# Second block's up projections: one 512-column matmul for the high and the low activations

## The reference

```python
for l in range(DEPTH_2):                      # DEPTH_2 = 2
    ...
    h = rmsnorm_2(x, norm_mlp[l])
    u = jax.nn.relu(jnp.einsum('bsd,df->bsf', h, w_up[l]))      # 2048 -> 8192
    x = x + jnp.einsum('bsf,fd->bsd', u * u, w_down[l])         # 8192 -> 2048
```

## Time and profile before

| | |
|---|---|
| Median of three runs | 3373.12 us (3364.39 to 3373.55) |
| Profiled execution, span from first to last instruction | 3372.1 us |
| TensorE busy (matmuls) | 3234.7 us, 96% |
| VectorE busy | 2239.3 us, 66% |
| ScalarE busy | 1423.9 us, 42% |
| Matmuls | 27278 |
| Mean granted clock of TensorE | 0.973 of full speed |

### The profile page before, as it was taken

The page is one execution under the profiler, slowest core; times in us unless marked ns, Lnnn a source line. Parts: engine busy times, 40 slices in busy tenths (PEclk is TensorE's granted clock), DMA queues, the critical chain, the costliest instruction groups (busy, mean ns, idle before and its releaser), DMA issues.

```text
span 3372.1 us, 63513 instructions
## 1 busy us (share of the span) xinstructions
PE 3234.7 (96%) x27278; PEld 3164.4 (94%) x27278; DVE 2239.3 (66%) x2341; ACT 1423.9 (42%) x1398; POOL 157.7 (5%) x292
## 2 busy tenths in 40 slices
PE   5999979999999999989999999999998999999998
PEld 5998879999999999978999999999987999999998
DVE  5898877666666677677655655567667756555655
ACT  3253334444444444545434343434454543434333
POOL 2111100000000000011000000000010000000000
PEclk6899989999999999999999999999999999999999
DMA  9788867666656644445555555555444555555553
GB/s 384 285 305 307 292 255 265 218 207 217 206 205 212 211 139 162 142 136 161 188 197 188 197 188 196 189 198 165 150 129 134 176 188 198 187 198 188 197 189 136
DMA packets 320749, 681.68 MB, mean 202 GB/s; under 512 B 14768, under 2 KB 21620, under 8 KB 320164
## 3 DMA queue, kind: packets, MB, share of 16 engines
q1 hardware_dynamic: 286272, 562.74, 49.6%
q0 software_dynamic: 31232, 109.07, 8.9%
q10 hardware_dynamic: 3108, 7.89, 0.6%
HBM read 677.47 MB, written 7.94 MB: 203 GB/s over the span
## 4 chain that ended last, share of the span: by engine, by line
PE 84%; DVE 9%; DMA 3%; issue 2%; ACT 2%; POOL 0%; ACTq 0%; DVEq 0%; POOLq 0%; SPq 0%
PE G L693 50%; PE Dn L693 32%; DVE w_lo L1260 2%; DVE ada_acc L1385 1%; PE Dn L696 1%; DMA ada_raw<-in_w_ada 1%; ACT w_hi L2209 1%; DMA zT<-in_w_ada 1%; DMA raw<-in_w_in 1%; DVE sq L1309 1%; DMA raw<-in_w_out 0%; DVE negmax L1676 0%; DVE s_sb L1669 0%; DVE sq L1984 0%; DVE s_sb L1673 0%
## 5 line engine op out<-in xcount | busy, mean ns | idle before, releaser
L693 PE MATMUL G<-h_hi,w_hi 128*128 128x256 f32 x5760 | 1620.0, 281 | 9.0 <-DVE w_lo L1260 4.7
L1260 DVE TENSOR_TENSOR w_lo<-raw,w_hi 128x2048 fp32r<-128x2048 f32 (+2 forms) x536 | 1219.1, 2275 | 602.7 <-ACT w_hi L2209 601.8
L2209 ACT CAST w_hi<-raw 128x2048 fp32r<-128x2048 f32 (+2 forms) x536 | 1017.3, 1900 | 1416.3 <-DMA raw<-in_w_down 427.4
L693 PE MATMUL G<-h_lo,w_hi 128*128 128x256 f32 x5760 | 1607.0, 279 | 0.0
L693 PE MATMUL G<-h_hi,w_lo 128*128 128x256 f32 x5760 | 1606.2, 279 | 0.0
L693 PEld LDWEIGHTS G<-h_hi,w_hi 128*128 128x128 f32 x5760 | 1094.3, 190 | 24.0 <-issue 19.7
L693 PEld LDWEIGHTS G<-h_lo,w_hi 128*128 128x128 f32 x5760 | 1094.5, 190 | 0.3
L693 PEld LDWEIGHTS G<-h_hi,w_lo 128*128 128x128 f32 x5760 | 1094.1, 190 | 0.0
L693 PE MATMUL Dn<-act_hi,w_hi 128*128 128x256 f32 x2752 | 762.1, 277 | 7.4 <-DVE act_lo L1802 7.4
L693 PE MATMUL Dn<-act_hi,w_lo 128*128 128x256 f32 x2752 | 761.5, 277 | 0.0
L693 PE MATMUL Dn<-act_lo,w_hi 128*128 128x256 f32 x2752 | 761.4, 277 | 0.0
(11 more groups left out here) (264 smaller groups left out, 1662.7 us busy)
## 6 DMA issues: line engine op xcount, KB each, us to landing
raw<-in_w_up SPq DMA_DIRECT2D x128, 1024.0 KB, 5.3
raw<-in_w_down SPq DMA_DIRECT2D x128, 1024.0 KB, 5.0
raw<-in_w_in SPq DMA_DIRECT2D x88, 1024.0 KB, 5.2
ada_raw<-in_w_ada POOLq DMA_DIRECT2D x120, 512.0 KB, 6.3
raw<-in_w_ffn_gate SPq DMA_DIRECT2D x44, 1024.0 KB, 5.0
raw<-in_w_ffn_up SPq DMA_DIRECT2D x44, 1024.0 KB, 5.1
raw<-in_w_ffn_down SPq DMA_DIRECT2D x44, 1024.0 KB, 5.0
raw<-in_w_o SPq DMA_DIRECT2D x32, 1024.0 KB, 5.0
```

Source lines behind the costliest of these rows:

```text
L693: return nc.tensor.matmul(o, lhsT, rhs, start=start, stop=stop, skip_group_check=True)
L1260: v.tensor_tensor(w_lo[j][:, 0:m], raw[j][:, 0:PIECE_K * n], w_hi[j][:, 0:m], ALU.subtract).then_inc(lo_done, 1)
L2209: s.copy(w_hi[j][:, 0:PIECE_K * n], raw[j][:, 0:PIECE_K * n]).then_inc(hi_done, 1)
```

## The change

`h_hi` and `h_lo` become the two halves of one tensor, and G[0] and G[1] become one PSUM tensor of four banks. In groups 1 to 15 of each layer the new `piece_joint` takes the place of `piece`: for each block of high weights one matmul passes both the high and the low activations, 512 columns, into a whole bank, one half for each; the low weights pass the high activations into the first half as before. A group so takes all four banks. On evacuation ScalarE first copies the second halves to `g_si` (`ff_low_part`), VectorE adds this to the first halves into `stage_p`, and a further VectorE instruction applies relu and rstd. Group 0 keeps the old form, and group 1 now waits until group 0 has been evacuated from G[1].

```diff
-        h_hi = sb("h_hi", [P, KT, T], F32R)
-        h_lo = sb("h_lo", [P, KT, T], F32R)
+        h_hl = sb("h_hl", [P, 2, KT, T], F32R)
+        h_hi, h_lo = h_hl[:, 0, :, :], h_hl[:, 1, :, :]
...
-        G = [ctx.enter_context(nc.psum_tensor(f"G{i}", [P, 4, T], F32)) for i in range(2)]
+        GG = ctx.enter_context(nc.psum_tensor("G", [P, 2, 4, T], F32))
+        G = [GG[:, i, :, :] for i in range(2)]
+        GJ = GG[:, :, :, :].rearrange("p g (f h) t -> p (g f) h t", h=2)
...
+            def piece_joint(quad, j, kts, first, last):
+
+                pe.wait_ge(lo_done, quad * 4 + (j + 1))
+                hi = w_hi[j][:, 0:PIECE_K * PIECE_N].rearrange("p (k n) -> p k n", k=PIECE_K)
+                lo = w_lo[j][:, 0:PIECE_K * PIECE_N].rearrange("p (k n) -> p k n", k=PIECE_K)
+                for kk in range(PIECE_K):
+                    for f in range(4):
+                        c = P * f
+                        mm(GJ[:, f, :, :], hi[:, kk, c:c + P], h_hl[:, :, kts + kk, :], first and kk == 0, False)
+                        i = mm(GJ[:, f, 0, :], lo[:, kk, c:c + P], h_hi[:, kts + kk, :], False, last and kk == PIECE_K - 1)
                 i.then_inc(pe_done, 1)
...
                                 pe.wait_ge(g_free[0], gb[0] + (i + 9))
-                            piece(quad, j, G[1 if first else 0], h_hi, h_lo, 4 * UP_ORDER[j], j == 0, j == 3)
+                                if isinstance(i, int):
+                                    pe.wait_ge(g_free[1], gb[1] + 11)
                             if first:
+                                piece(quad, j, G[1], h_hi, h_lo, 4 * UP_ORDER[j], j == 0, j == 3)
                                 run_hooks(48 + j)
+                            else:
+                                piece_joint(quad, j, 4 * UP_ORDER[j], j == 0, j == 3)
...
                         dve.wait_ge(a_lo, an + i)
-                        b = 1 if isinstance(i, int) and i == 0 else 0
-                        v.scalar_tensor_tensor(out=stage_p[:, :, :], in0=G[b][:, :, :], scalar=0.0,
-                                               in1=rstd[:, :].unsqueeze(1).broadcast_to([P, 4, T]),
-                                               op0=ALU.max, op1=ALU.mult).then_inc(g_free[b], 1)
...
+                        dve.wait_ge(ff_half, l * (FF2_GROUPS - 1) + i)
+                        v.tensor_tensor(stage_p[:, :, :], GJ[:, :, 0, :], g_si[:, :, :], ALU.add).then_inc(g_free[0], 1)
+                        dve.wait_ge(g_free[0], gb[0] + i + 10)
+                        v.scalar_tensor_tensor(out=stage_p[:, :, :], in0=stage_p[:, :, :], scalar=0.0, in1=spread_rstd,
+                                               op0=ALU.max, op1=ALU.mult).then_inc(ff_rel, 1)
...
+                    def ff_low_part(i, pieces):
+                        act.wait_ge(pe_done, pieces)
+                        s.copy(g_si[:, :, :], GJ[:, :, 1, :]).then_inc(ff_half, 1)
+
                     def ff_square(i):
...
-                            act.wait_ge(g_free[0], gb[0] + i + 10)
+                            act.wait_ge(ff_rel, l * (FF2_GROUPS - 1) + i)
...
                         for n in range(8):
+                            if n == 0:
+                                ff_low_part(k + 1, lp + k * 8 + 56)
                             hi(lq + k * 2 + (14 + (n + 1) // 4), (n + 1) % 4)
```

More of the change, by code:

```diff
@@ L464, in two_stage_kernel @@
         ff_p = sem("hidden_product_done")
+        ff_rel = sem("hidden_rectified")
+        ff_half = sem("hidden_low_part_copied")
         a_hi = sem("hidden_hi")
@@ L717, in piece @@
                             i.then_inc(misc_w, 1)
+                i.then_inc(pe_done, 1)
+            def piece_joint(quad, j, kts, first, last):
[7 more added lines that the diff above has]
+                        i = mm(GJ[:, f, 0, :], lo[:, kk, c:c + P], h_hi[:, kts + kk, :], False, last and kk == PIECE_K - 1)
                 i.then_inc(pe_done, 1)
@@ L2111, in ff_relu @@
                         dve.wait_ge(a_lo, an + i)
-                        b = 1 if isinstance(i, int) and i == 0 else 0
-                        v.scalar_tensor_tensor(out=stage_p[:, :, :], in0=G[b][:, :, :], scalar=0.0,
-                                               in1=rstd[:, :].unsqueeze(1).broadcast_to([P, 4, T]),
-                                               op0=ALU.max, op1=ALU.mult).then_inc(g_free[b], 1)
+                        spread_rstd = rstd[:, :].unsqueeze(1).broadcast_to([P, 4, T])
+                        if isinstance(i, int) and i == 0:
+                            v.scalar_tensor_tensor(out=stage_p[:, :, :], in0=G[1][:, :, :], scalar=0.0, in1=spread_rstd,
+                                                   op0=ALU.max, op1=ALU.mult).then_inc(g_free[1], 1)
+                            return
+                        dve.wait_ge(ff_half, l * (FF2_GROUPS - 1) + i)
[3 more added lines that the diff above has]
+                                               op0=ALU.max, op1=ALU.mult).then_inc(ff_rel, 1)
                     an = l * FF2_GROUPS + FF1_GROUPS
@@ L2704, in _ @@
                     for n in range(8):
+                        if n == 0:
+                            ff_low_part(FF2_GROUPS - 1, pc)
                         if n < 7 or more:
```

## The result

The changed kernel takes 3419.19 us against 3372.19 before (medians of four runs each, 3413.11 to 3424.40 and 3364.39 to 3373.55): ratio 1.0148, 95% interval 1.0135 to 1.0161. It is slower by some 50 us, beyond the whole range of the prediction.

A forecast was written before the change was run, and what follows sets the result against it. TensorE's matmuls were taken to bound the kernel. Saving -23.0, handover +13.8 and layers' starts +4.3 gave -4.9 us on a span of 3372.1, 3367.2, so 3368 against the runs' median; 8-in-10 range 3354 to 3384.

The forecast's parts named there:

- What bounds the kernel: TensorE, busy 96% of the span; the end moves only with its matmul rate and its waits.
- The saving, -23.0 us: Changed up groups: 1920 places, each saving 12.0 ns by one matmul and weight load fewer.
- Small end: the 6.6 ns stick to every matmul: Lower bound of the saving: one dropped matmul gives 6.6 ns a place, 12.7 us in all.
- Both ends of my bracket: Bounds of the saving in the up groups: 6.6 to 17.3 ns a place, 12.7 to 33.2 us.
- the transposes' 109.4 ns: Spacing of 128x128 transposes at full clock, taken as the single matmul's floor at the large end of the saving.
- A floor for a pair of weight load and matmul: On TensorE, weight load plus matmul seems to take at least 109 to 113 ns whatever it streams.
- The rule of the Trainium skill: Warm matmuls follow at N/2.4 + 2.5 ns: 15.0 ns saved a place, 28.8 us, sum 3361.
- The handover, +13.8 us: Behind each up group ScalarE's copy delays the cast and two down pieces: 0.46 us a group, 30 groups.
- The layers' starts, +4.3 us: Group 1 waits until G[1] is evacuated: 2.15 us in each of two layers; bounds 4.3 to 7.5.
- the second late piece: Down piece pc+2 waits for Dn[0] to be emptied: 0.46 us late in all, including pc+1's 0.16.
- The rivals: Four cases for the time: 3368 (chance 0.38), 3358 (0.28), 3378 (0.18), 3390 (0.16).
- Rival 4: VectorE's queue before Dn[0] hangs on ScalarE's copy; at 0.85 us a group +17.1 us, 3390; chance 0.16.

The follow-up runs named there:

- run 5: Changed kernel, low weights also pass high and low activations, so every up-group matmul has 512 columns: 3631.17 us, ratio 1.0769.
- run 9: Changed kernel, in each up piece all 16 joint matmuls first, then its 16 single ones: 3403.94 us, ratio 1.0094.
- run 3: Changed kernel, ScalarE casts piece pc+1 before it copies the low halves: 3403.12 us, ratio 1.0088.
- run 6: Changed kernel, joint matmul split into two of 256 columns and ScalarE's cast ahead of its copy: 3374.94 us, ratio 1.0016.
- run 11: Kernel before the change, plus one unused 128-column matmul between down and up group in each of 28 rounds: 3383.16 us, ratio 1.0031.
- run 12: Kernel before the change, plus one unused 256-column matmul between down and up group in each of 28 rounds: 3385.09 us, ratio 1.0038.
- run 1: Changed kernel, joint matmul split into two of 256 columns, evacuation and waits kept: 3393.23 us, ratio 1.0065.
- run 8: Changed kernel, joint matmul split into two of 256 columns, cast before copy, group 1's wait for G[1] 8 of 16 places later: 3368.71 us, ratio 0.9998.
- run 2: Changed kernel, high and low activations of a row block laid side by side, 512 contiguous columns: 3418.52 us, ratio 1.0148.
- run 4: Changed kernel, within a row block four joint matmuls first, then the four single ones: 3407.36 us, ratio 1.0102.
- run 10: Changed kernel, joint matmuls kept, cast before copy, late wait for G[1] in group 1, 16 joint then 16 single matmuls: 3400.18 us, ratio 1.0086.

## Why the prediction was wrong, point by point

- **What bounds the kernel**: right. TensorE's matmuls set the time, and what changed is their rate and their pauses.
- **The saving, -23.0 us**: this is the step that failed. "Small end: the 6.6 ns stick to every matmul" was taken for a bound and was none. Both ends of my bracket read the difference between 106.7 and 113.3 ns as something that a matmul pays once, so fewer matmuls could only save. Runs 5 and 9 show that a 512-column matmul pays at least twice: 228.8 ns at best, 15.5 over its 213.3 ns of columns, and 233 to 234 in other stretches; alternating with a single one it takes 235. The dropped matmul gave back nothing. Cast-first kernels differ by the joint matmul alone in runs 3 and 6: 44.37 - 43.51 = 0.86 us a round, 30 x 0.86 = +25.8 us where -23.0 stood. The larger part of this loss is the rate, as far as run 9's rows tell (no run had the fast rate throughout): at their best a place would take 228.8 + 113.1 = 342 ns, 2 ns or 4 us in all over the kernel before, and the other 11 ns a place, some 21 us, were lost where the alternating stream ran at the slow rate throughout. No term of the prediction stood for that. As I named it, "the prediction is wrong if a 512-column matmul takes longer than its two halves"; it had no price and no chance among the rivals, and that is why the range missed. The rows could not refute it: none had 512 columns, and the transposes' 109.4 ns, of tensors declared float32 and not fp32r, were no evidence about a long stream. A floor for a pair of weight load and matmul is not refuted: the extra matmul of 128 columns cost no less than that of 256 (runs 11 and 12). What failed is the step from it, that above the floor a matmul costs little more than its columns.
- **The rule of the Trainium skill**: N/2.4 + 2.5 ns ("TensorE: Matmul & The Clock Gate", "Back-to-back issue gap"), which that section gives for an isolated matmul, is 215.8 ns for 512 columns. No run showed it for these fp32r operands; 228.8 was the lowest. The measurements decide: here the gap rule is no basis for a saving. (The sum by it is 3362, not 3361: 3373.1 - 10.7.)
- **The handover, +13.8 us**: right in place, order and size. By the rounds of runs 1 and 6, 43.96 - 43.51 = 0.45 us a group, 13.5 us. Its make-up was wrong: half of it is pauses (0.21 us), half the slower rate that follows the first pause. In the changed kernel itself the cast first gives 0.54 us.
- **The layers' starts, +4.3 us**: under-sized. The pause of 2.07 us was right (2.15 forecast); the fall of the clock behind it, which I left out at 1.6 us a layer, came in both layers, 1.5 us each: 7.2 us. Less the 0.5 us a layer by which group 1 was slower in the kernel before too, this is 6.2 us; run 8 against run 6 gives 6 us.
- **The sum**: 25.8 + 13.5 + 6.2 = 45.5 us. Some 3 us more for the 30 groups come when both costs are there together (44.91 against 43.51 is 1.40 us, and 0.86 + 0.45 = 1.31): in 10 of 28 rounds of the changed kernel the slow rate outlasts the second late piece, in none of run 1, 0.42 us each. Measured by the ratio 50, by the spans 48.2.
- **The rivals**: none held. Rival 4 had the right sign by the wrong place: Dn[0] cost what was forecast for it, and the point from which it would decide was never reached.

Open stays why a matmul carries more beside its columns when it has 512 of them, and why there are two rates (113.3 and 117.7 ns, 229 and 233 to 235) at one granted clock. The layout of the operand (run 2) makes no difference, and the banks and their readers don't slow 256-column matmuls (run 1). Mixing lengths isn't needed for the extra 2 ns (run 5), but the order of the lengths does decide how long TensorE stays at the slow rate: always when they alternate, part of the time in runs 4, 5 and 9.

## What to carry to other kernels

Before merging matmuls to save what they cost beyond their columns, find out whether that surcharge is per matmul or per column; a row at another length and of the same data type is needed, and where none exists the bracket must reach to the other sign. When a new reader of a finished PSUM tile is put at the head of an engine's queue, count what that queue fed ahead of time: here one copy ahead of one cast used up 6.6 us of lead, and moving it behind the cast cost nothing and gave all of it back. In a kernel that keeps TensorE at its rate, a short pause or a stray matmul can cost several times its own length, and a small delay inside such a slow stretch may cost nothing, so that remedies tested one by one need not add up (run 10).

## What was not expected of the hardware

- fp32r matmuls of 256 columns run either every 113.3 or every 117.7 ns at a granted clock of 1.00. All 28 extra matmuls and many pauses were followed by the slow rate; behind the one at 2901.98 it lasted some 11.4 us, about 96 matmuls. After a second pause 5.7 us later the rate was the fast one in 18 of 28 rounds (2918.75 above) and still the slow one in 10. 28 extra matmuls of 128 or of 256 columns cost 0.54 and 0.55 us each.
- fp32r matmuls of 512 columns have two rates too, 229 and 233 ns in a stream of their own (run 5). No stretch of them came down to twice 113.3 ns.
- A pause of 2.07 us was followed by a granted clock of 0.50 in both layers, where one of 0.8 us before 2631.38 was not (1.00 granted from 2631.3 to 2640).
